# Conditioning in four blocks of 256 channels inside the first projections, and gates stored as nine rows

## The chip, the cores and the metric

The program runs on one NeuronCore of a Trainium2 chip. The metric is the device time of one execution in microseconds (us), the median of several runs. The engines are TensorE (PE in the rows; PEld is its weight load), VectorE (DVE), ScalarE (ACT), GpSimd (POOL) and SyncE (SP), each with a queue of its own, worked off in order. They wait for one another at semaphores.

## The reference

Two layers over a residual stream of width 1024, for one prompt of 1024 tokens and 8 samples of 16 tokens (1152 tokens, 9 tiles of 128). Before each of three stages the stream is normalized and modulated with a shift and a scale per sequence; the two layers also multiply their output with a gate per sequence. All come from a conditioning vector c (one for the prompt, eight for the samples: nine rows).

```
ada_mod(c, w, b)   = silu(c) @ w + b                     # w is 1024 x 3072: shift | scale | gate
modulate(x, g, shift, scale) = rms_norm(x, g) * (1 + scale) + shift
layer 0: h = modulate(x);  q, k, v, g = h @ w_in (1024 x 6144);  retention, head norm, * silu(g)
         x = x + gate * (o @ w_out)
shared:  h = modulate(x);  k, v, log forget gates = h @ kv_w
layer 1: h = modulate(x);  q, g = h @ w_in;  forgetting attention;  x = x + gate * (o @ w_out)
```

All weights are float32. A float32 product is done as three in float32r: each operand is a high part (rounded) and a low part (the rest), and hi·hi, hi·lo and lo·hi are added.

## The kernel before

**condition** (line 234) is a program block of its own with a barrier at its end. It clears c_rows and a bias tile on GpSimd (L280, L281), loads c and an identity, applies SiLU, transposes c to `pr.cT` (L309), and multiplies it with the shift and scale columns of a_ada_w: eight slices of 128 rows by 2048 columns (1 MB each, L273, four buffers), four products of 32 output rows for each slice, side by side in the array's column groups (L315). The bias is added (L332), four transposes turn the rows (L320), and `modulation` (L222) writes mod_b (shift) and mod_a ((1 + scale) times the norm's gain). The first weight chunk qk[0] is loaded between (`load_parts`, L167) and split into high (ScalarE, L196) and low (VectorE, L208). Then the nine x tiles come in (L276), ScalarE sums their squares (L301), and a root (L303) and a reciprocal (L340) give rstd for all nine.

**intake** (line 344) makes q, k and v of layer 0. GpSimd multiplies 128 channels of all tokens with rstd (L472) into one of two buffers xs. `turn(d)` on TensorE transposes them (L532, nine transposes) into PSUM, `modulated(d)` on VectorE applies mod_a and mod_b (L623 to L627) into ht, ScalarE casts ht to hT_hi (L499) and VectorE subtracts for hT_lo (L634). Turn 1 uses spare banks of another PSUM tensor, so turns 0 and 1 don't wait for each other. Meanwhile `products` (L542) of the first weight chunk run step by step over the eight d for AHEAD = 5 output tiles at once, in five PSUM banks. In this loop (L589) TensorE's queue has turn(d+2) first and then the products of d; VectorE's has modulated(d+1) and then the low part of d. After it come the other tiles of chunk 0 and seven more chunks, in the order of the code. The outputs go to DRAM scratch. From line 440 on, the rest of the conditioning (`side_steps`, L551) is done between these tiles: the gates of both layers and the shift and scale of the other two norms. SyncE waits for the last low part (L444) before it loads the rotary tables and the first side slices.

**Gates before.** `side_end(0)` after tile (4, 4) multiplies the nine gate rows with a table of zeros and ones, sel_gate (L578, eight products of 128x512), which repeats them for the 128 rows of a tile. VectorE copies each out (L677) and GpSimd stores it (L488) into the scratch tensor "gate" of (128, 2, 2, 1024). The trunk loads it with one transfer each for the prompt and the samples (L1025, L1039), the tail likewise (L1812, L1811).

The order of the queues is written out by hand; there is no planner.

Of the kernel before, what the change touches and what calls it, by code (L numbers as in the profile page):

```python
# [29 lines left out]
P = 128  # L30
# [23 lines left out]
def tables():  # L54
# [17 lines left out]
    sel_gate = np.zeros((P, 2, 4, P))  # L72
    for j in range(4):
        sel_gate[BR * j + DEC_BATCH, 0, j, :] = 1
        for b in range(DEC_BATCH):
            sel_gate[BR * j + b, 1, j, b * DEC_SEQ:(b + 1) * DEC_SEQ] = 1
# [9 lines left out]
    for r in range(2):  # L86
# [4 lines left out]
             sel_gate=sel_gate, sel_bias=sel_bias, mask=mask, sel_group=sel_group, mask_s=mask_s)  # L91
# [3 lines left out]
class Program:  # L95


    def __init__(self, nc, ctx, dram, table):
        self.nc, self.ctx, self.dram, self.table = nc, ctx, dram, table

        self.raw = self.sb("w_raw", [P, 2, KS, CW])
        self.w_hi = self.sb("w_hi", [P, 2, KT, CW], F32R)
# [6 lines left out]
        self.rstd_ready = self.sem("rstd_ready")  # L109
# [124 lines left out]
def condition(pr, x, x_rows, weight):  # L234


    nc = pr.nc
    dr = pr.dram
    xv = x[:, :].rearrange("p (t d) -> p t d", t=TILES)
    with ExitStack() as ctx:  # L240
        sb = lambda n, s, dt=F32: ctx.enter_context(nc.sbuf_tensor(n, s, dt))
        ps = lambda n, s: ctx.enter_context(nc.psum_tensor(n, s, F32))
        sem = ctx.enter_context(semaphores(nc, "ada_"))
        c_rows = sb("c_rows", [BR, D])
        c_silu = sb("c_silu", [BR, D])
        w = sb("ada_w_sb", [P, 4, 4, CW])
        bias = sb("ada_bias", [P, CW])
        rows = sb("ada_rows", [P, CW])
        squares = sb("squares", [P, 2, D])
        stat = sb("ada_stat", [P, 3, TILES])  # L250
        ps_c = ps("ps_c", [P, 512])
        ps_ada = ps("ps_ada", [P, 512])
        ps_t = ps("ps_t", [P, 512])
        in_landed, c_ready, b_zero, b_landed = sem("in_landed"), sem("c_ready"), sem("b_zero"), sem("b_landed")
        s_silu, c_turned, cT_ready = sem("s_silu"), sem("c_turned"), sem("cT_ready")
        w_landed = [sem(f"ada_landed{i}") for i in range(4)]
        x_landed = [sem(f"x_landed{i}") for i in range(3)]
        w_read, rows_ready, turned = sem("ada_read"), sem("rows_ready"), sem("ada_turned")
        sq_done, me_done, rt_done = sem("sq_done"), sem("me_done"), sem("rt_done")
        block = ctx.enter_context(nc.Block())  # L260

        @block.sync
        def _(sp):
            sp.wait_ge(c_ready, 1)
            sp.dma_start(c_rows[0:DEC_BATCH], dr["c_sample"]).then_inc(in_landed, 16)
            sp.dma_start(c_rows[DEC_BATCH:DEC_BATCH + 1], dr["c_prompt"]).then_inc(in_landed, 16)
            sp.dma_start(pr.ident[:, :], pr.table["ident"]).then_inc(in_landed, 16)
            for k in range(KT):
                if k >= 4:
                    sp.wait_ge(w_read, k - 3)  # L270
                if k == 4:
                    load_parts(pr, sp, weight, 0, 0)
                sp.dma_start(w[:, k % 4], dr["a_ada_w"][k * P:(k + 1) * P, 0:4 * CW].rearrange("p (j c) -> p j c", j=4)).then_inc(w_landed[k % 4], 16)  # L273
            load_parts(pr, sp, weight, 0, 1)
            for t in range(TILES):
                sp.dma_start(xv[:, t], x_rows(t)).then_inc(x_landed[t // 3], 16)  # L276

        @block.gpsimd
        def _(pool):
            pool.memset(c_rows[:, :], 0.0).then_inc(c_ready, 1)  # L280
            pool.memset(bias[:, :], 0.0).then_inc(b_zero, 1)  # L281
            pool.wait_ge(b_zero, 1)
            for j in range(4):
                pool.dma_start(bias[BR * j:BR * j + 9, :], dr["a_ada_b"][0:1, j * CW:(j + 1) * CW].to_broadcast([9, CW])).then_inc(b_landed, 16)
            with nc.allow_non_contiguous_dma(reason="channel gains, once"):
                for m, g in enumerate(("a_norm_g", "kv_norm_g", "b_norm_g")):
                    pool.dma_start(pr.norm_g[:, m, :], dr[g].rearrange("a (k p) -> p (a k)", p=P)).then_inc(b_landed, 16)
                pool.dma_start(pr.gn_g[:, :, :], dr["a_gn_g"].rearrange("a (n k p) -> p (a n) k", p=P, k=KT)).then_inc(b_landed, 16)

        @block.scalar  # L290
        def _(act):
            act.wait_ge(in_landed, 48)
            act.activation(c_silu[:, :], c_rows[:, :], ACT.Silu).then_inc(s_silu, 1)
            for sub in range(SUBS):
                split_hi(pr, act, 0, 0, sub)
            for t in range(TILES):
                if t % 3 == 0:
                    act.wait_ge(x_landed[t // 3], 48)
                if t:
                    act.wait_ge(sq_done, t)  # L300
                act.activation(squares[:, t % 2], xv[:, t], ACT.Square, accum_out=stat[:, 0, t:t + 1]).then_inc(sq_done, 1)  # L301
            act.wait_ge(me_done, 1)
            act.activation(stat[:, 2, :], stat[:, 1, :], ACT.Sqrt).then_inc(rt_done, 1)  # L303

        @block.tensor
        def _(pe):
            pe.wait_ge(s_silu, 1)
            for k in range(KT):
                ins = pe.transpose(ps_c[:, k * BR:(k + 1) * BR], c_silu[:, k * P:(k + 1) * P], pr.ident[0:BR, 0:BR])  # L309
            ins.then_inc(c_turned, 1)  # L310
            pe.wait_ge(cT_ready, 1)
            for k in range(KT):
                pe.wait_ge(w_landed[k % 4], 16 * (k // 4 + 1))
                for j in range(4):
                    ins = pe.matmul(ps_ada[BR * j:BR * (j + 1), :], pr.cT[:, k, :], w[:, k % 4, j, :],  # L315
                                    start=k == 0, stop=k == KT - 1, tile_position=(0, BR * j), skip_group_check=True)
                ins.then_inc(w_read, 1)
            pe.wait_ge(rows_ready, 1)
            for c in range(4):
                ins = pe.transpose(ps_t[:, c * P:(c + 1) * P], rows[:, c * P:(c + 1) * P], pr.ident[:, :])  # L320
            ins.then_inc(turned, 1)

        @block.vector
        def _(dve):
            dve.sem_inc(pr.raw_split, 2)
            dve.wait_ge(c_turned, 1)
            dve.tensor_copy(pr.cT[:, :, :], ps_c[:, 0:KT * BR]).then_inc(cT_ready, 1)
            for sub in range(2):
                split_lo(pr, dve, 0, 0, sub)
            dve.wait_ge(b_landed, 8 * 16)  # L330
            dve.wait_ge(w_read, KT)
            dve.tensor_tensor(rows[:, :], ps_ada[:, :], bias[:, :], ALU.add).then_inc(rows_ready, 1)  # L332
            dve.wait_ge(turned, 1)
# [1897 lines left out]
```

## Time and profile before

| | us |
|---|---|
| median of 3 runs (1793.59 to 1796.32) | 1795.57 |
| the profiled execution | 1794.28 |
| its span | 1792.5 |
| TensorE matmuls busy | 1724.7 (96%) |
| VectorE busy | 698.6 (39%) |
| ScalarE busy | 564.4 (31%) |
| GpSimd busy | 343.2 (19%) |

The span is the time from the first to the last instruction in the profiled execution; a busy share is taken of it. Rows give start and duration in us; a mean duration in a row of groups is in ns. The matmuls are pipelined, so the durations of two that follow each other overlap; the distance of their starts, or the chain of waits, tells what one costs. A float32 matmul (not float32r) is recorded as two instructions.

### The profile page before, as it was taken

What the parts mean: (1) busy time and instruction counts of PE and PEld (TensorE: products, weight loads), DVE (VectorE), ACT (ScalarE), POOL (GpSimd) and SP (SyncE); (2) the same over time, 40 slices, a digit from 0 to 9 for tenths busy, and PEclk for the clock granted to TensorE, in tenths of its full rate; (3) what the DMA queues carried; (4) which work ended last, traced back from release to release, by engine and by line L of the source; (5) the groups of instructions that cost most, each with busy time, mean ns of one, the idle gap of its engine ahead of it and who ended that gap; (6) DMA issues with size and microseconds to landing.
All of it is one profiled execution on the core that took longest, in us unless ns stands there. A gap on an engine that the chain in (4) does not pass through costs nothing.

```text
span 1792.5 us, 21860 instructions
## 1 busy us (share of the span) xinstructions
PE 1724.7 (96%) x8477; PEld 1325.6 (74%) x8477; DVE 698.6 (39%) x1429; ACT 564.4 (31%) x924; POOL 343.2 (19%) x413
## 2 busy tenths in 40 slices
PE   3699999999999999999999999999999998999998
PEld 0699998677876666666668888888788876777776
DVE  1654443211124444435433434645553115444432
ACT  2321111111133434434431224425222134344432
POOL 1311111100012323222222224404200000110000
PEclk9999999999999999999999999999999999999999
DMA  9064444542345645466562311332323645332200
GB/s 336 32 233 163 150 162 152 195 149 105 102 160 183 217 157 191 169 194 221 178 243 72 118 36 36 120 110 78 105 77 124 179 145 163 115 105 71 71 25 36
DMA packets 122568, 245.41 MB, mean 137 GB/s; under 512 B 15445, under 2 KB 50417, under 8 KB 121442
## 3 DMA queue, kind: packets, MB, share of 16 engines
q1 hardware_dynamic: 101202, 176.13, 30.8%
q0 software_dynamic: 21264, 67.88, 9.8%
q8 instruction: 68, 1.11, 0.3%
q14 instruction: 34, 0.28, 0.1%
HBM read 170.95 MB, written 73.02 MB: 136 GB/s over the span
## 4 chain that ended last, share of the span: by engine, by line
PE 93%; DVE 1%; ACT 1%; issue 1%; DMA 0%; POOL 0%; DVEq 0%; ACTq 0%; POOLq 0%
PE trunk_ps L1075 39%; PE in_ps_o L546 11%; PE in_ps_o L542 11%; PE tail_ps L1927 6%; PE tail_ps L1918 4%; PE tail_ps L1885 3%; PE trunk_ps L1101 3%; PE trunk_ps L1116 3%; PE tail_ps L1895 2%; PE trunk_ps L1111 2%; PE trunk_ps L1177 1%; PE tail_ps L1861 1%; PE in_ps_o L567 1%; PE trunk_ps L1145 1%; PE trunk_ps L1088 1%
## 5 line engine op out<-in xcount | busy, mean ns | idle before, releaser
L1075 PE MATMUL trunk_ps<-w_hi,hT_hi 128*128 128x512 f32 x1008 | 410.4, 407 | 0.0
L1075 PE MATMUL trunk_ps<-w_hi,hT_lo 128*128 128x512 f32 x1008 | 401.1, 398 | 0.0
L1075 PE MATMUL trunk_ps<-w_lo,hT_hi 128*128 128x512 f32 x1008 | 397.3, 394 | 0.0
L1075 PEld LDWEIGHTS trunk_ps<-w_hi,hT_hi 128*128 128x128 f32 x1008 | 189.3, 188 | 59.4 <-issue 17.6
L1075 PEld LDWEIGHTS trunk_ps<-w_lo,hT_hi 128*128 128x128 f32 x1008 | 189.5, 188 | 49.3 <-issue 5.0
L1075 PEld LDWEIGHTS trunk_ps<-w_hi,hT_lo 128*128 128x128 f32 x1008 | 189.2, 188 | 44.5
L208 DVE TENSOR_TENSOR w_lo<-w_raw,w_hi 128x1024 fp32r<-128x1024 f32 x80 | 101.6, 1272 | 296.3 <-ACT w_hi L196 291.1
L542 PE MATMUL in_ps_o<-hT_hi,w_hi 128*128 128x384 f32 x384 | 131.5, 342 | 4.6 <-DVE hT_lo L634 4.6
L542 PE MATMUL in_ps_o<-hT_hi,w_lo 128*128 128x384 f32 x384 | 130.0, 338 | 0.0
L542 PE MATMUL in_ps_o<-hT_lo,w_hi 128*128 128x384 f32 x384 | 130.0, 338 | 0.0
L546 PE MATMUL in_ps_o<-w_hi,hT_hi 128*128 128x512 f32 x288 | 115.2, 400 | 0.0
L546 PE MATMUL in_ps_o<-w_hi,hT_lo 128*128 128x512 f32 x288 | 113.9, 396 | 0.0
L546 PE MATMUL in_ps_o<-w_lo,hT_hi 128*128 128x512 f32 x288 | 113.2, 393 | 0.0
L196 ACT CAST w_hi<-w_raw 128x1024 fp32r<-128x1024 f32 x80 | 83.5, 1044 | 36.2 <-DMA w_raw<-in_a_w_in 36.2
L1410 POOL TENSOR_TENSOR room<-room 128x512 f32<-128x512 f32 x36 | 46.2, 1282 | 241.4 <-ACT room L1313 241.4
L1420 POOL TENSOR_TENSOR room<-room 128x512 f32<-128x512 f32 x36 | 56.4, 1568 | 139.9 <-DVE room L1601 139.9
L2016 ACT COPY tail_pT<-tail_ps 128x512 f32<-128x512 f32 (+3 forms) x104 | 46.3, 473 | 116.2 <-PE tail_ps L1895 116.1
L542 PEld LDWEIGHTS in_ps_o<-hT_hi,w_hi 128*128 128x128 f32 x384 | 72.8, 190 | 11.8 <-issue 10.3
L518 ACT COPY room<-in_ps_o 128x512 f32<-128x512 f32 x36 | 21.1, 587 | 184.9 <-PE in_ps_o L546 184.9
L2036 POOL TENSOR_TENSOR room<-room 128x512 f32<-128x512 f32 x16 | 20.2, 1264 | 279.1 <-DVE room L2125 279.1
L542 PEld LDWEIGHTS in_ps_o<-hT_lo,w_hi 128*128 128x128 f32 x384 | 72.9, 190 | 0.0
L542 PEld LDWEIGHTS in_ps_o<-hT_hi,w_lo 128*128 128x128 f32 x384 | 72.9, 190 | 0.0
(243 smaller groups left out, 2662.2 us busy)
## 6 DMA issues: line engine op xcount, KB each, us to landing
w_raw<-in_a_w_in SPq DMA_DIRECT2D x96, 256.0 KB, 3.0
room<-in_state_ret SPq DMA_DIRECT2D x64, 256.0 KB, 4.1
out_state_sample<-room POOLq DMA_DIRECT2D x64, 256.0 KB, 4.4
room<-in_b_ada_w SPq DMA_DIRECT2D x24, 512.0 KB, 6.2
scratch_qkT<-room POOLq DMA_DIRECT2D x48, 192.0 KB, 2.2
scratch_v<-room POOLq DMA_DIRECT2D x36, 256.0 KB, 2.6
room<-scratch_v SPq DMA_DIRECT2D x36, 256.0 KB, 4.4
scratch_o<-room POOLq DMA_DIRECT2D x36, 256.0 KB, 3.4
```

Source lines behind the costliest of these rows:

```text
L196: act.copy(pr.w_hi[:, slot, sub * KS:(sub + 1) * KS, :], pr.raw[:, sub % 2]).then_inc(pr.hi_done, 1)
L208: dve.tensor_tensor(pr.w_lo[:, slot, sub * KS:(sub + 1) * KS, :], pr.raw[:, sub % 2], pr.w_hi[:, slot, sub * KS:(sub + 1) * KS, :].bitcast ...
L542: ins = pe.matmul(ps_o[:, bank(c, t), 0:NB3], w[:, s, k, w0:w0 + P], h[:, k, n * NB3:(n + 1) * NB3], start=k + m == 0, stop=k == KT - 1 an ...
L546: ins = pe.matmul(ps_o[:, bank(c, t), :], h[:, k, t * P:(t + 1) * P], w[:, s, k, :], start=k + m == 0, stop=k == KT - 1 and m == 2)
L1075: ins = pe.matmul(ps[:, bank, :], h[:, k, t * P:(t + 1) * P], w[:, (C0 + j) % 2, k, :], start=k + m == 0, stop=k == KT - 1 and m == 2)
L1101: ins = pe.matmul(ps[:, PS_U + a, :], k_tok[:, c % 2, a * P:(a + 1) * P], v[:, n % 3], start=True, stop=True)
L1116: ins = pe.matmul(ps[:, PS_O, :], q[:, a, :], state[:, a, :], start=False, stop=a == 1)
L1420: pool.tensor_tensor(x1[:, t, cols_], x1[:, t, cols_], tmp[:, :], ALU.add).then_inc(added, 1)
L1885: ins = pe.matmul(ps[:, pair + a, 0:w], qT[:, s % 2, i, :], kT[:, n, a * CW:a * CW + w], start=True, stop=True)
L1918: ins = pe.matmul(ps[:, V, 0:DH], pT[:, x, y * P:(y + 1) * P], v_of(b)[:, n, :], start=b == 0, stop=b == blocks[u] - 1)
L1927: ins = pe.matmul(ps[:, bank, :], a[:, h, :], w[:, c, h, :], start=h + m == 0, stop=h == FH - 1 and m == 2)
L2016: act.copy(pT[:, x, 0:w], ps[:, TURN + place["p", u, x] % 2, 0:w]).then_inc(pt_ready, 1)
```

## The change

The block `condition` and its barrier are gone; intake does its work. The conditioning comes in four blocks m of 256 channels: the 256 shift and the 256 scale columns, side by side as 512, for all 1024 rows of the weight (2 MB, four transfers with runs of 1 KB), in two buffers that lie where the second weight chunk will be split to. One block is eight products: column group j sums k = j and k = 4 + j, and four small products with a 128x32 table "fold" add the groups and turn the rows at once. x is loaded first and scaled in place by VectorE, three tiles at a time. The splits of the first weight chunk into low parts go from VectorE to GpSimd. There is one PSUM buffer for turns, AHEAD is 4, and in the loop over d the turn stands behind the products. The gates are stored as nine rows, and the loads repeat them. Three pairs of semaphores are merged. What follows is the core.

```diff
+    "gate": (2, DEC_BATCH + 1, D)          # scratch, was (P, 2, 2, D)
-    AHEAD = 5
+    AHEAD = 4
+    BLOCK = 2 * P
@@ intake, sync
+            def ada_block(m):
+                if m >= 2:
+                    sp.wait_ge(*summed[m - 2])
+                for e in range(2):
+                    rows = slice(4 * e * P, 4 * (e + 1) * P)
+                    for h in range(2):
+                        cols = slice(h * D + m * BLOCK, h * D + (m + 1) * BLOCK)
+                        sp.dma_start(pr.ada[m % 2][:, 4 * e:4 * e + 4, h * BLOCK:(h + 1) * BLOCK],
+                                     dr["a_ada_w"][rows, cols].rearrange("(k p) c -> p k c", p=P)).then_inc(ada_in[m % 2], 16)
+            sp.wait_ge(*cleared)
...
+            for t in range(TILES):
+                sp.dma_start(xv[:, t], x_rows(t)).then_inc(x_in[t // 3], 16)
+            ada_block(0)
+            load_sub(pr, sp, chunks[0], 0, 0)
+            load_sub(pr, sp, chunks[0], 0, 1)
+            ada_block(1)
+            ada_block(2)
+            load_sub(pr, sp, chunks[0], 0, 2)
+            ada_block(3)
+            load_sub(pr, sp, chunks[0], 0, 3)
             load_parts(pr, sp, chunks[1], 1, 0)
@@ gpsimd
-            pool.wait_ge(pr.rstd_ready, 1)
-            for d in range(KT):
-                if d >= 2:
-                    pool.wait_ge(turned, d - 1)
-                pool.tensor_tensor(xs[:, d % 2]..., xv[:, :, d * P:(d + 1) * P], pr.rstd..., ALU.mult)
+            pool.wait_ge(*cleared)
...
+            for sub in range(SUBS):
+                split_lo(pr, pool, 0, 0, sub)
...
+                    if (c, t) == gates_at:
+                        pool.wait_ge(rows_read, 1)
+                        for j in range(4):
+                            dst = dr["gate"][j // 2, :, (j % 2) * CW:(j % 2 + 1) * CW].rearrange("b (a c) -> b a c", a=4)
+                            pool.dma_start(dst, side_rows[0][BR * j:BR * j + DEC_BATCH + 1]).then_inc(gate_stored, 16)
@@ scalar (squares of t wait for x_in[t // 3]; their output goes to PSUM)
+            for t in range(TILES):
+                squares(t)
+                if t in (3, 6):
+                    root(t // 3 - 1)
+            root(2)
+            for sub in range(2):
+                split_hi(pr, act, 0, 0, sub)
             for d in range(KT):
                 act.wait_ge(ht_ready, d + 1)
                 act.copy(hT_hi[:, d, :], ht[:, d % 2, :]).then_inc(hi_done, 1)
+                if d in (1, 3):
+                    split_hi(pr, act, 0, 0, 2 + d // 2)
@@ tensor
+            def ada(m):
+                pe.wait_ge(ada_in[m % 2], 64 * (m // 2 + 1))
+                if m:
+                    pe.wait_ge(*mods_out[m - 1])
+                for e in range(2):
+                    for j in range(4):
+                        ins = pe.matmul(ps_side[BR * j:BR * (j + 1), :], pr.cT[:, 4 * e + j, :], pr.ada[m % 2][:, 4 * e + j, :],
+                                        start=e == 0, stop=e == 1, tile_position=(0, BR * j), skip_group_check=True)
+            def fold_rows(m):
+                pe.wait_ge(*rows_out[m])
+                for a in range(4):
+                    ins = pe.matmul(ps_side[:, a * BR:(a + 1) * BR], ada_rows[:, a * P:(a + 1) * P], fold, start=True, stop=True, ...)
             def turn(d):
-                dst = turned_in(d)
-                pe.wait_ge(xs_ready, d + 1)
-                if d >= 2:
-                    pe.wait_ge(ht_ready, d - int(d == 2))
+                if d == 0:
+                    pe.wait_ge(*x_scaled)
+                else:
+                    pe.wait_ge(ht_ready, d)
@@ side_end
-                if r == 0:
-                    for n in range(8):
-                        if n >= 2:
-                            pe.wait_ge(g_read, n - 1)
-                        pe.matmul(ps_t[:, n % 2, :], sel_gate[:, n // 4, n % 4, :], side_rows[0], start=True, stop=True).then_inc(g_done, 1)
@@ tensor, main
+            ada(0)
+            fold_rows(0)
             turn(0)
             turn(1)
-            pe.wait_ge(pr.raw_split, SUBS + 2)
+            ada(1)
+            fold_rows(1)
             for d in range(KT):
+                pe.wait_ge(h_ready, d + 1)
+                pe.wait_ge(pr.raw_split, d // KS + 1 + 2)
+                for t in range(AHEAD):
+                    products(0, t, d)
+                if d in (1, 3):
+                    ada(2 + d // 2)
+                if d in (2, 4):
+                    fold_rows(1 + d // 2)
                 if d + 2 < KT:
                     turn(d + 2)
-                if d == 0:
-                    pe.wait_ge(ht_ready, 2)
-                pe.wait_ge(h_ready, d + 1)
-                for t in range(AHEAD):
-                    products(0, t, d)
@@ vector (rows: the bias; mods: mod_b and mod_a of two d; low: hT_lo)
+            dve.memset(c_rows, 0.0).then_inc(prepared, 1)
+            dve.memset(ada_bias, 0.0).then_inc(prepared, 1)
...
+            for g in range(3):
+                scaled_rows(g)
+            rows(0)
+            mods(0)
             modulated(0)
-            for d in range(KT):
+            modulated(1)
+            rows(1)
+            low(0)
+            mods(1)
+            for d in range(1, KT):
                 if d + 1 < KT:
                     modulated(d + 1)
...
+                low(d)
+                if d in (1, 3):
+                    rows(2 + d // 2)
+                if d in (2, 4):
+                    mods(1 + d // 2)
@@ trunk and tail, sync
-            sp.dma_start(gate[:, 1], dr["gate"][:, 0, 1]).then_inc(gate_in[1], 16)
+            for b in range(DEC_BATCH):
+                sp.dma_start(gate[DEC_SEQ * b:DEC_SEQ * (b + 1), 1], dr["gate"][0, b:b + 1, :].to_broadcast([DEC_SEQ, D])).then_inc(gate_in[1], 16)
-            sp.dma_start(gate_s[:, :], dr["gate"][:, 1, 1]).then_inc(gate_in, 16)
+            for b in range(DEC_BATCH):
+                sp.dma_start(gate_s[DEC_SEQ * b:DEC_SEQ * (b + 1), :], dr["gate"][1, b:b + 1, :].to_broadcast([DEC_SEQ, D])).then_inc(gate_in, 16)
```

## Rows read from the trace of the kernel before

**Rows 1.** First part of the page: busy time, share of the span, instructions.
```profile
PE 1724.7 (96%) x8477; PEld 1325.6 (74%) x8477; DVE 698.6 (39%) x1429; ACT 564.4 (31%) x924; POOL 343.2 (19%) x413
```

**Rows 2.** Chain of waits, 60 to 96 us: start, us, what.
```profile
62.25 3.20 DVE hT_lo L634
65.58 5.14 PE in_ps_o L542 x15
...
71.87 2.61 PE in_ps_o L542 x15
...
85.92 1.00 PE in_ps_t L532 x9
86.94 0.29 DVE room L623
87.24 0.98 DVE room L624
88.22 0.45 DVE room L625
88.67 0.20 DVE room L627
88.87 1.28 DVE hT_lo L634
...
90.19 5.86 PE in_ps_o L542 x31
```

**Rows 3.** Timeline, 0 to 62 us: start, us, engine, line, what, [idle before].
```profile
0.74 0.94 POOL L280 MEMSET c_rows<- 32x1024 f32 x1 [0.29 <-POOLq L2216]
1.63 0.52 POOL L281 MEMSET ada_bias<- 128x512 f32 x1
...
32.80 1.93 PE L315 MATMUL ps_ada<-ada_w_sb,cT 128*32 128x512 f32 x8 [0.58 <-DMA ada_w_sb<-in_a_ada_w]
34.88 0.69 DVE L332 TENSOR_TENSOR ada_rows<-ps_ada,ada_bias 128x512 f32<-128x512 f32 x1 [9.76 <-PE ps_ada L315]
35.63 1.11 PE L320 MATMUL ps_t<-ident,ada_rows 128*128 128x128 f32 x4 [0.89 <-DVE ada_rows L332]
...
50.76 1.28 ACT L303 ACT_TABLE_LOAD   x1
55.61 2.18 PE L532 MATMUL in_ps_t<-ident,room 128*128 128x128 f32 x9 [18.87 <-POOL room L472]
60.28 1.36 PE L532 MATMUL in_ps_t<-ident,room 128*128 128x128 f32 x9 [0.42 <-DVE room L627]
```

**Rows 4.** Stretches: busy us and count by engine, granted clock, DMA share, GB/s.
```profile
0.00:10.00 10.00, 2.12 (x16) 1.16 (x16) 0.42 (x1) 2.34 (x2) 7.70 (x14) 1.00 0.66 221
10.00:16.00 6.00, 2.81 (x15) 0.20 (x8) 0.00 (x0) 0.00 (x0) 0.00 (x0) 1.00 1.01 223
16.00:24.00 8.00, 3.87 (x16) 0.40 (x16) 1.33 (x2) 2.09 (x2) 0.00 (x0) 1.00 1.03 388
31.00:34.00 3.00, 2.42 (x16) 0.20 (x8) 0.00 (x0) 0.00 (x0) 0.00 (x0) 1.00 1.07 353
64.10:70.90 6.80, 5.32 (x17) 5.25 (x18) 4.53 (x6) 1.15 (x1) 0.12 (x1) 0.50 0.00 0
1494.30:1497.70 3.40, 1.72 (x14) 1.37 (x12) 2.24 (x10) 1.41 (x5) 0.00 (x0) 1.00 0.69 122
```

**Rows 5.** Groups of instructions by shape: count, busy us, mean ns.
```profile
L301 ACT ACTIVATE squares<-room 128x1024 f32<-128x1024 f32 x9 | 9.5, 1056 | 3.6 <-DMA room<-in_x_prompt 3.1 <-DMA room<-in_x_sample 0.3
L1375 POOL TENSOR_TENSOR room<-room,mod_b 128x1024 f32<-128x1024 f32 x16 | 37.3, 2329 | 45.7 <-DVE room L1536 45.7
```

**Rows 6.** Chain of waits, 300 to 345 us: the gate products.
```profile
321.18 0.87 PE in_ps_t L578 x2
...
329.23 11.20 PE in_ps_o L546 x48
```

**Rows 7.** SyncE's queue in the timeline: the load behind gate_s and gate in the tail.
```profile
1483.40 0.43 SPq L1778 DMA_DIRECT2D room<-out_v_prompt  x1
```

More of the change, by code:

```diff
@@ L71, in tables @@
                                EPS * np.exp(-2 * (i + 1.0) * g), EPS * np.exp(-2 * (loc + 1.0) * g)], 1) for g in lg], 1)
[L72 to L76, printed above, removed]
     sel_bias = np.zeros((4, 4, BR))
@@ L101, in __init__ @@
         self.raw = self.sb("w_raw", [P, 2, KS, CW])
+        with ExitStack() as below:
+            below.enter_context(nc.sbuf_tensor("below_w", [P, KT * CW], F32))
+            ada_0 = below.enter_context(nc.sbuf_tensor("ada_w0", [P, KT, CW], F32))
+            below.enter_context(nc.sbuf_tensor("between_w", [P, KT * CW], F32))
+            ada_1 = below.enter_context(nc.sbuf_tensor("ada_w1", [P, KT, CW], F32))
+        self.ada = [ada_0, ada_1]
         self.w_hi = self.sb("w_hi", [P, 2, KT, CW], F32R)
@@ L231, in modulation @@
     return ins
[L234 to L333, printed above, removed]
-            modulation(pr, dve, 0, ps_t[:, :])
-            for sub in range(2, SUBS):
-                split_lo(pr, dve, 0, 0, sub)
-            dve.wait_ge(sq_done, TILES)
-            dve.tensor_scalar(stat[:, 1, :], stat[:, 0, :], 1.0 / D, EPS, ALU.mult, ALU.add).then_inc(me_done, 1)
-            dve.wait_ge(rt_done, 1)
-            dve.reciprocal(pr.rstd[:, :], stat[:, 2, :]).then_inc(pr.rstd_ready, 1)
@@ L344, in intake @@
-def intake(pr, room, weights, after):
+def intake(pr, room, x_rows, weights, after):
     nc, dr = pr.nc, pr.dram
@@ L359, in bank @@
     def bank(c, t):
-        if c == 0 and t < AHEAD:
-            return t
         return t % 4 if c < ROT else t % 3
@@ L411, in intake @@
         side_tab, side_c_ready, side_used, rows_read = sem("side_tab"), sem("side_c_ready"), sem("side_used"), sem("rows_read")
-        g_done, g_read, side_turned, side_mod = sem("g_done"), sem("g_read"), sem("side_turned"), sem("side_mod")
-        gate_stored = [sem(f"gate_stored{i}") for i in range(3)]
-        def turned_in(d):
-            return ps_o[:, AHEAD - 3:AHEAD, :] if d == 1 else ps_t[:, :, :]
+        side_turned, side_mod, gate_stored = sem("side_turned"), sem("side_mod"), sem("gate_stored")
         def slot_of(c, t):
@@ L452, in _ @@
                 sp.dma_start(side_bias[:, r, :], dr[f"{m}_ada_b"][0:1, 0:4 * CW].rearrange("o (j c) -> (o j) c", c=CW)).then_inc(side_tab, 16)
-            sp.dma_start(sel_gate[:, :, :, :], pr.table["sel_gate"].rearrange("p (a b c) -> p a b c", a=2, b=4)).then_inc(side_tab, 16)
             for c in range(CHUNKS):
@@ L613, in _, with scaled_rows, rows, mods @@
         def _(dve):
+            def scaled_rows(g):
+                part = slice(3 * g, 3 * g + 3)
+                dve.wait_ge(*squared[g])
+                dve.tensor_scalar(stat[:, 1, part], stat[:, 0, part], 1.0 / D, EPS, ALU.mult, ALU.add).then_inc(prepared, 1)
+                dve.wait_ge(*root_of[g])
+                dve.reciprocal(pr.rstd[:, part], stat[:, 2, part]).then_inc(prepared, 1)
+                dve.wait_ge(*inverted[g])
+                for t in range(3 * g, 3 * g + 3):
+                    dve.tensor_scalar(xv[:, t], xv[:, t], pr.rstd[:, t:t + 1], None, ALU.mult).then_inc(prepared, 1)
+            def rows(m):
+                if m == 0:
+                    dve.wait_ge(bias_in, 6 * 16)
+                dve.wait_ge(*summed[m])
+                dve.tensor_tensor(ada_rows, ps_side, ada_bias[:, m, :], ALU.add).then_inc(prepared, 1)
+            def mods(m):
+                dve.wait_ge(*folded[m])
+                new = ps_side[:, 0:4 * BR].rearrange("p (a b) -> p a b", a=4)[:, :, 0:DEC_BATCH + 1]
+                dve.tensor_copy(pr.mod_b[0][:, 2 * m:2 * m + 2, :], new[:, 0:2])
+                for e in range(2):
+                    ins = dve.tensor_scalar(pr.mod_a[0][:, 2 * m + e, :], new[:, 2 + e], 1.0, pr.norm_g[:, 0, 2 * m + e:2 * m + e + 1], ALU.add, ALU.mult)
+                ins.then_inc(prepared, 1)
             def modulated(d):
-                z, src = ht[:, d % 2, :], turned_in(d)
+                z = ht[:, d % 2, :]
                 dve.wait_ge(turned, d + 1)
+                dve.wait_ge(*mods_out[d // 2])
                 if d >= 2:
```

140 lines of the change are left out of this document (85 added, 55 removed).

## Prediction

> **What bounds the kernel now.** I read the page's first part before anything else: matmuls are busy for 1724.7 us of 1792.5 [rows 1], so whatever stands still or is redundant on TensorE is what can be won. The chain of waits comes next, because it says where TensorE isn't what is waited for. Of the two places that this change touches, the first is the head of the program. TensorE does nothing that lasts before its first product of the projections at 65.58 [rows 2]; ahead of it lie, one after the other, the conditioning's eight loads and products (the last from 32.80), the squares, a root, the row scaling on GpSimd, and two sets of transposes from 55.61 [rows 3]. From 65.58 the eight steps d of the first five tiles run. The turn of step d+2 stands ahead of the products of step d, so VectorE works on the next step beneath the products: in the chain a step is almost wholly TensorE's (2.61 of products, 1.00 of transposes), and only for the last turn does VectorE's row of work come into sight, 86.94 to 90.15 [rows 2]. The last low part ends at 90.15, and 30 products of that phase are left from 90.19; at 0.174 us each (2.61 / 15) they end at 95.4. The second place is the gate expansion at 321: the chain leaves the value products at 321.18 and is back in them at 329.23 [rows 6].
>
> **Front of the program, step by step.** I rebuild the new order from rows of the old.
> *Clearing.* SyncE now waits for two clears on VectorE, 1024 and 2048 columns. VectorE clears nothing in this trace; the nearest rows are GpSimd's, 0.94 us for 1024 and 0.52 for 512 [rows 3], so about 3.1 us from 0.74: SyncE starts at 3.9, not at 1.7 behind the first clear alone, 2.2 us later. Bounds: half of it if VectorE clears twice as fast, and 3.1 as taken. The Trainium skill (VectorE: DVE Perf Modes, "Zero memsets can be issued as uint32 (trn2)") gives a clear one cycle per element whatever the type, which by its 0.96 GHz would be 3.2 us; no run here shows it yet.
> *x.* It is 4.7 MB and now comes first. The old stream had moved 2.2 MB by 10 us and 3.55 by 16 (223 GB/s while the gains' tiny elements are on the queues), then ran at 388 [rows 4]: 4.85 MB at 19.4, plus 2.2 for the late start is 21.6. Squares are 1.06 us each [rows 5], 1.2 with the readout of their sum (nine of them in 11 us); three can run only after the last third of x, with the root's table load (1.28) [rows 3] already behind: roots at 26.3, reciprocal, then three scalings on VectorE. A 128x1024 multiply by a column isn't in the trace; 768 columns out of PSUM took 0.98 [rows 2], so at most 1.3 each, and perhaps half: x is scaled by 28.5 to 30.5.
> *First block.* 2.1 MB in 1 KB runs at the 353 GB/s that 31 to 34 us shows, where the slices are mostly such runs [rows 4]: 21.6 + 5.9 = 27.5. Its eight products are two of the old groups of four (1.94 each) [rows 3]: 31.3, later than the scaling, which so costs nothing. Adding the bias 0.69, fold about 0.7 (the four transposes were 1.11), four small VectorE operations 0.65 to 0.7: the fold ends at 32.8 and turn(0), 2.18 us at the low clock level, at 35.0. Modulation is 0.29 + 0.98 + 0.45 + 0.20 in the old chain; two of its operations are merged, so 1.75: 36.8. turn(1) now has to wait for that, since there is one PSUM buffer: 39.1. Block 1 (27.5 + two slices of weights 3.0 + 5.9 = 36.4) is there; its products end at 43.0, bias 43.7, low part 1.28: the first projection product starts at **45.1**. All TensorE times in this are those of the 1.2 GHz level. At 2.4 GHz from turn(0) on it would be 41.8. I take 43.5, the middle: 22 us ahead of 65.58.
> *The eight steps.* Here the change gives most of it back. turn(d+2) now stands behind products(d). low(d) stands behind modulated(d+1) on VectorE, which needs turn(d+1), which stands behind products(d-1). So nothing overlaps: products 12 x 0.174 = 2.09, turn 1.00, modulation 1.75, low part 1.28, releases 0.05 = 6.15 us, six times = 36.9. Within it TensorE also gets blocks 2 and 3 (16 products, twice 1.9 at full clock: half of 3.87) and two folds (0.9 together). The bias additions and the mods on VectorE lie beside turns. The last two products take 4.2. Sum from 43.5: 43.5 + 36.9 + 3.8 + 0.9 + 4.2 = 89.3. One tile fewer is ahead than in the old phase: 24 x 0.174 = 4.2, so 93.5 against 95.4: **-1.9**, at the full clock.
> *GpSimd's four weight splits.* A 128x1024 of its own took 2.33 us [rows 5]; they end at some 47 and 63 us for the last two, between two low parts, so I cost them at nothing. If one meets a low part, the row is hT_lo at 3.20 in the chain beside GpSimd's scaling, against 1.28 alone [rows 2]: +1.9 each, bounds 0 and 3.8.
>
> **TensorE's clock in this phase.** TensorE idles for 0.05 + 1.75 + 1.28 + 0.05 = 3.1 us in each step. In the old trace it stood still from 61.6 [rows 3] to 65.6 and the granted clock was 0.50 from 64.1 to 70.9, the 1.2 GHz level; it was 1.00 again afterwards, and stayed there over pauses of 1 to 1.5 us, as in 1494.3 to 1497.7 with 1.72 us of products in 3.40 [rows 4]. A pause of 3.1 lies between these. A step at half clock costs 2.09 + 0.96 more, a block 1.9, a fold 0.45: 27 us if all are, 0 if none. But a step at the low level holds 6 us of unbroken TensorE work, as much as brought the level back in the old trace, so it should return about once a step. I take two of eight, **+6**.
> The Trainium skill warns here (TensorE: Matmul & The Clock Gate, "HAM oscillation — how this bites in real kernels"): a loop whose products are shorter than the wait behind them starts every round throttled. By that rule all eight steps would be slow; the old trace agrees only in that its one pause of 4 us did so. It is the second rival below.
>
> **The gates.** Eight products of 128x512 and the waits between them go: 329.23 - 321.18 = **-8.05** on the chain [rows 6]. The sel_gate load, eight copies and eight 256 KB stores go too, beside TensorE: nothing more. Four small stores take their place on GpSimd. Reading nine rows costs SyncE seven more issues for gate[:,1] and seven for gate_s, at the 0.43 us of the issue in [rows 7]: 3.0 us each on that queue. Queued behind the first are three x tiles that the residual needs much later, behind the second the values load at 1483.40 for the tail's next step. Bounds 0 and 6; I take **+0.5**, as both look covered.
> Merged semaphores and the moved PSUM bank cost nothing: same order, same instructions.
>
> **Sum.** -1.9 + 6 - 8.05 + 0.5 = -3.5 us. The profiled execution took 1794.28 (span 1792.5), so 1790.8; the median of the runs is 1795.57, 1.3 higher, and the changed kernel's median should be **1792.1**. About 0.2%, 3.6 us, is what a measurement of this kernel can tell from none.
>
> **Rivals.**
> *The clock stays up (0.22).* For it: the pause is shorter than the one that brought it down, and blocks 2 and 3 fill two steps. Then the start is 41.8 and nothing is added: -3.6 - 8.05 + 0.5 = -11.2, **1784.4**.
> *The clock drops in most steps (0.17), the slower side.* One mechanism, TensorE's 3.1 us pause. From a start of 45.1 the full-clock balance is -7.9, and each slow step adds 3.05: it turns to a loss with the third slow group and is a measurable one from the fourth. Five give +7.4, **1803**; all eight with blocks and folds 1815. Against it: 6 us of work in a row each time.
> *The blocks come late (0.16).* If 1 KB runs move at the 223 GB/s of 10 to 16 us instead of 353, block 0 lands at 31.0 and block 1, with the weight slices between, at 45.1; its products end at 49.0 instead of 43.0. That adds 6: **1798**. Against it: 223 was beside tiny elements, which are gone by then.
> Forecast itself: 0.45, own range 1788.5 to 1796.
>
> **How the numbers follow.** Faster: all of the first rival (0.22) and 0.24 of the forecast, which lies right at the bound; 0.46. Same: 0.21 of the forecast and 0.11 of the late blocks, 0.32. Slower: 0.17 and 0.05, 0.22. The range 1783 to 1802 holds the forecast, most of the first rival, nearly all of the third and half of the second.
>
> **What would show it.** First product at 41 to 46. Between product groups of the first eight steps: starts 6.2 us apart where granted clock is 1.00, about 9 where 0.50, with VectorE's modulated and low rows in the chain each time. Twelve products a group. No gate products between the value tiles. What would make it wrong: a low part beside a GpSimd split at 3 us, a first product after 47, a granted clock at one level throughout, or a wait in the tail on the later values load.

## The result: 9 us slower, and where they went

Five runs of the changed kernel gave a median of 1802.59 us (1797.13 to 1803.32), five of the kernel before, on the same chip, 1793.59 (1792.06 to 1796.32): a ratio of 1.0035, 95% interval 1.0019 to 1.0050. (The ratio is an estimate from all the runs; that of the two medians alone is 1.0050. The same holds for the ratios below.) I forecast 1792.1, 3.5 us faster; it is 9 us slower and just outside the range (1783 to 1802). The profiled execution is the fastest of the five (1797.13, span 1795.3), so a second profile stands beside it below, of a run at 1804.91 (span 1803.1), which is 1.3 us above the median of its own batch.

The first part of the page of after, the answer to [rows 1]:

```profile
PE 1720.6 (96%) x8489; PEld 1331.0 (74%) x8489; DVE 696.1 (39%) x1429; ACT 564.2 (31%) x926; POOL 331.4 (18%) x401
```

TensorE is busy 4 us less in a span that is 3 us longer, so it stands still more. The chain of waits of after, 28 to 125 us, answers to [rows 2]. Line numbers have moved: L512 is the old L542 (products), L502 the old L532 (turn), L484 a block's products, L492 the fold, L626 to L629 `modulated`, L634 the low part, L531 the first side step.

```profile
29.24 3.25 PE in_ps_o L484 x16
...
43.83 2.38 PE in_ps_o L512 x12
46.22 1.00 PE in_ps_t L502 x9
47.21 0.02 issue
47.23 0.29 DVE room L626
47.52 1.25 DVE room L627
48.78 0.53 DVE room L629
49.31 1.28 DVE hT_lo L634
50.59 0.04 issue
50.63 2.35 PE in_ps_o L512 x12
52.98 1.85 PE in_ps_o L484 x16
54.84 1.15 PE in_ps_t L502 x9
...
59.07 3.91 PE in_ps_o L512 x12
62.99 0.81 PE in_ps_o L492 x8
...
67.91 2.98 PE in_ps_o L512 x12
70.89 2.83 PE in_ps_o L484 x16
...
85.24 3.16 PE in_ps_o L512 x12
88.40 1.80 PE in_ps_t L502 x9
...
93.28 26.82 PE in_ps_o L512 x144
120.10 0.99 PE in_ps_o L531 x8
```

The serial step is there as drawn: products, turn, three operations of `modulated`, the low part, and only then the next products; of VectorE's work only a block's bias addition and mods lie beside TensorE's. What is new against the forecast is that the same twelve products take 2.35, 2.98, 3.16 or 3.91. The stretches say why. The last column but two is the granted clock; the last row is the whole loop, the other four are the half-clock stretches in and behind it, each 3.4 us (a fifth, 38.7 to 42.1, lies ahead of it):

```profile
59.10:62.50 3.40, 3.40 (x11) 3.40 (x12) 0.00 (x0) 0.78 (x1) 2.37 (x1) 0.52 0.00 0
69.40:72.80 3.40, 3.40 (x18) 1.58 (x20) 0.00 (x0) 0.00 (x0) 0.00 (x0) 0.51 0.00 0
86.40:89.80 3.40, 3.40 (x15) 3.31 (x15) 0.00 (x0) 0.00 (x0) 0.00 (x0) 0.52 0.00 0
93.30:96.70 3.40, 3.40 (x11) 3.40 (x12) 1.24 (x1) 0.00 (x0) 0.00 (x0) 0.51 0.31 96
43.80:93.30 49.50, 30.53 (x175) 24.58 (x175) 21.06 (x36) 8.91 (x8) 4.71 (x2) 0.90 0.25 81
```

Each step has a pause of 3.1 us, and where the clock falls it comes back within the same step, as forecast, but it falls more than twice: four times from 59 to 97 here. Three of the loop's six groups show it, the one at 59.07 from its start, those at 67.91 and 85.24 only 1.5 and 1.2 us in. A group that meets the whole stretch loses 1.56 (3.91 - 2.35).

Read at fixed places of the program, with the second profile of the changed kernel and the one of the experiment that holds the clock up (all in us from the span's start):

| | before | after | changed again | clock held up |
|---|---|---|---|---|
| first projection product | 65.6 | 43.8 | 47.3 | 45.6 |
| last two product groups begin | 90.2 | 93.3 | 99.5 | 90.0 |
| first side step | 112.5 | 120.1 | 126.7 | 115.2 |
| trunk's first product | 512.7 | 512.3 | 518.9 | 507.4 |
| tail's first transposes | 1463.1 | 1464.2 | 1470.9 | 1459.2 |
| tail's last output product begins | 1787.7 | 1790.5 | 1798.3 | 1784.9 |
| span | 1792.5 | 1795.3 | 1803.1 | 1789.7 |

The front of the changed kernel gains 18 to 22 us at the first product and has lost 8 to 14 at the first side step. From there to the trunk every kernel with the new gates takes 392.2 to 392.3 instead of 400.2: 8.0 us. Behind the trunk's start the changed kernel loses 1.6 us ahead of the tail and 1.7 to 2.9 in it. The profiles show half clock again there: 919.3 to 922.7 and 1496.1 to 1502.9 in after, 925.6 to 929.0 and 1502.5 to 1512.7 in the second profile, where the profile of before has none in either place.

### The profile page after: what moved, and what is told of

Read it like the earlier page. It is cut to its first block, busy times and chain, and to the rows that moved or that the text cites. A ratio compares the mean times of both kernels' runs of the same rounds, so it can differ in the third digit from the quotient of the medians.

```text
span 1795.3 us, 21868 instructions
## 1 busy us (share of the span) xinstructions
PE 1720.6 (96%) x8489; PEld 1331.0 (74%) x8489; DVE 696.1 (39%) x1429; ACT 564.2 (31%) x926; POOL 331.4 (18%) x401
## 4 chain that ended last, share of the span: by engine, by line
PE 94%; DVE 2%; ACT 1%; issue 1%; SPq 1%; DMA 1%; DVEq 0%; ACTq 0%
PE trunk_ps L1091 39%; PE in_ps_o L512 12%; PE in_ps_o L516 11%; PE tail_ps L1944 6%; PE tail_ps L1935 4%; PE tail_ps L1902 3%; PE trunk_ps L1117 3%; PE trunk_ps L1132 3%; PE tail_ps L1912 2%; PE trunk_ps L1127 2%; PE trunk_ps L1193 1%; PE tail_ps L1878 1%; PE in_ps_o L537 1%; PE trunk_ps L1161 1%; PE trunk_ps L1104 1%
## 5 line engine op out<-in xcount | busy, mean ns | idle before, releaser
L1091 PEld LDWEIGHTS trunk_ps<-w_hi,hT_hi 128*128 128x128 f32 x1008 | 189.8, 188 | 59.1 <-issue 17.5
L1091 PEld LDWEIGHTS trunk_ps<-w_hi,hT_lo 128*128 128x128 f32 x1008 | 189.6, 188 | 45.1
L208 DVE TENSOR_TENSOR w_lo<-w_raw,w_hi 128x1024 fp32r<-128x1024 f32 x76 | 96.8, 1275 | 282.9 <-ACT w_hi L196 277.7
L512 PE MATMUL in_ps_o<-hT_hi,w_hi 128*128 128x384 f32 x384 | 132.5, 345 | 19.1 <-DVE hT_lo L634 19.1
L512 PE MATMUL in_ps_o<-hT_lo,w_hi 128*128 128x384 f32 x384 | 130.9, 341 | 0.0
L512 PE MATMUL in_ps_o<-hT_hi,w_lo 128*128 128x384 f32 x384 | 130.9, 341 | 0.0
L512 PEld LDWEIGHTS in_ps_o<-hT_hi,w_hi 128*128 128x128 f32 x384 | 73.4, 191 | 26.6 <-DVE hT_lo L634 20.7
L1426 POOL TENSOR_TENSOR room<-room 128x512 f32<-128x512 f32 x36 | 46.3, 1286 | 241.4 <-ACT room L1329 241.4
L196 ACT CAST w_hi<-w_raw 128x1024 fp32r<-128x1024 f32 x80 | 83.5, 1044 | 13.4 <-DMA w_raw<-in_a_w_in 13.4
L1436 POOL TENSOR_TENSOR room<-room 128x512 f32<-128x512 f32 x36 | 56.5, 1568 | 141.4 <-DVE room L1617 141.4
L467 ACT COPY room<-in_ps_o 128x384 f32<-128x384 f32 x48 | 23.0, 481 | 161.5 <-PE in_ps_o L512 158.5
L512 PEld LDWEIGHTS in_ps_o<-hT_hi,w_lo 128*128 128x128 f32 x384 | 73.7, 192 | 0.0
L512 PEld LDWEIGHTS in_ps_o<-hT_lo,w_hi 128*128 128x128 f32 x384 | 73.6, 192 | 0.0
```

The lines of the kernel that those rows point to most:

```text
L196: act.copy(pr.w_hi[:, slot, sub * KS:(sub + 1) * KS, :], pr.raw[:, sub % 2]).then_inc(pr.hi_done, 1)
L208: dve.tensor_tensor(pr.w_lo[:, slot, sub * KS:(sub + 1) * KS, :], pr.raw[:, sub % 2], pr.w_hi[:, slot, sub * KS:(sub + 1) * KS, :].bitcast ...
L512: ins = pe.matmul(ps_o[:, bank(c, t), 0:NB3], w[:, s, k, w0:w0 + P], h[:, k, n * NB3:(n + 1) * NB3], start=k + m == 0, stop=k == KT - 1 an ...
L1091: ins = pe.matmul(ps[:, bank, :], h[:, k, t * P:(t + 1) * P], w[:, (C0 + j) % 2, k, :], start=k + m == 0, stop=k == KT - 1 and m == 2)
L1426: pool.tensor_tensor(o_t[:, n % 2], o_t[:, n % 2], g_t[:, :], ALU.mult).then_inc(gated, 1)
L1436: pool.tensor_tensor(x1[:, t, cols_], x1[:, t, cols_], tmp[:, :], ALU.add).then_inc(added, 1)
```

## Experiments

Seven kernels in two batches, each batch beside the kernel before on the same chip: 1793.86 (17 runs) for the first four, 1794.81 (7 runs) for the last three.

**The changed kernel again.** No edit.

> The changed kernel once more, for a second profile and more runs. Its first profiled run was 1797.1 and the median 1802.6, a spread of 6 us where the kernel before has 4. If that spread is TensorE's clock falling in other steps of the loop and later, this profile shows the same order and the same instructions with half-clock stretches in other places or of other length, and the time goes with the number of them, about 1.7 us for each stretch of 3.4 us in which TensorE is the one waited for.

1803.59 (1797.00 to 1805.60, 6 runs), ratio 1.0043 (1.0027 to 1.0058). The loss repeats. Its chain of waits:

```profile
29.30 3.68 PE in_ps_o L484 x16
...
33.82 1.91 PE in_ps_o L492 x8
...
41.73 3.56 PE in_ps_o L484 x16
...
47.32 3.27 PE in_ps_o L512 x12
...
55.36 3.87 PE in_ps_o L512 x12
...
65.32 3.91 PE in_ps_o L512 x12
...
74.16 2.35 PE in_ps_o L512 x12
...
82.60 3.91 PE in_ps_o L512 x12
...
91.43 3.09 PE in_ps_o L512 x12
...
99.50 27.24 PE in_ps_o L512 x144
```

Five of the six groups in the loop are slow in part, and so is the work ahead of it: the fold took 1.91 here and 1.08 at 33.34 in after. The loop took 52.2 us against 49.5 in after. It is the same program: how often the clock falls differs from one execution to the next. That the times, from 1797 to 1806, spread with it fits these two profiles; the other runs have none.

**The gate part alone, on the kernel before.** The whole gate part of the diff (four row stores on GpSimd for eight products, copies and stores; loads that repeat the rows), nothing of the conditioning:

```diff
-                if r == 0:
-                    for n in range(8):
...
-                        pe.matmul(ps_t[:, n % 2, :], sel_gate[:, n // 4, n % 4, :], side_rows[0], ...)
...
+                    if (c, t) == gates_at:
...
+                        for j in range(4):
...
+                            pool.dma_start(dst, side_rows[0][BR * j:BR * j + DEC_BATCH + 1]).then_inc(gate_stored, 16)
```

> The kernel before with the gate part of the change alone: nine rows stored, repeated by the loads, no expansion products. Theory A: the chain loses the 8.0 us between 321.2 and 329.2 and nothing else moves, so 8 us less than before, about 1785.5. Theory C (the additional loads on SyncE's queue and the reads of single rows cost what the products gave): 0 to 3 us less, 1791 to 1794.

1787.28 (1785.84 to 1788.19, 5 runs), ratio 0.9960 (0.9948 to 0.9972). That is 5 to 9 us of gain, 6.6 by the medians, with 392.3 us from the first side step (111.7) to the trunk (504.0): the 8.0 of the table. It is less than 8 in all because this profile too has half clock in the tail (6.8 us of it, 1486.4 to 1493.2), which takes 1.8 us longer than in before; so that isn't the new front's doing alone. The gates do what was forecast, and the rest of the change costs about 16 (1803.6 - 1787.3) where I had it at +4.

**Clock held up by filler products.** After, with 14 products of 128x384 behind each of the six turns, into a bank that is free then. They read what is there and are thrown away; they stand in the pause that TensorE has anyway:

```diff
...
+                    pe.wait_ge(*[mods_out[1], rows_out[2], mods_out[2], rows_out[3], mods_out[3], mods_out[3]][d])
+                    for _ in range(FILL):
+                        pe.matmul(ps_side[:, 0:NB3], pr.w_hi[:, 0, 0, 0:P], hT_hi[:, 0, 0:NB3], start=True, stop=True)
```

> The changed kernel with 14 products of 128x384 added behind each of the six turns in the loop, into a free PSUM bank; their result is not used. They fill 2.4 us of TensorE's pause of 3.4 us at the full clock. Theory A with the clock as its second part: the granted clock stays at 1.00 from the second step on, the steps lose their half-clock share, and the time falls by 5 to 7 us against the changed kernel, to about 1796, with less spread between runs; the serial order itself stays (steps of 6.8 us). If the clock has no part in it: 0 to +2 us, since the fillers only take up idle time.

1792.25 (1791.29 to 1795.79, 11 runs), ratio 0.9991 (0.9982 to 0.9999): 11.3 us under the changed kernel in the same batch, with more work in it. First the loop's stretch, then three pieces of the chain of waits:

```profile
45.60:90.00 44.40, 40.36 (x259) 35.01 (x259) 20.73 (x36) 8.91 (x8) 4.76 (x2) 1.00 0.25 80
```

```profile
45.61 2.35 PE in_ps_o L513 x12
...
62.84 0.81 PE in_ps_o L493 x8
...
89.98 25.23 PE in_ps_o L513 x144
```

The granted clock is 1.00 through the loop, against 0.90 in after and 0.84 in its second profile. The order of the work is untouched, so this prices the clock by itself. The two profiles of that batch differ by 13.4 (1804.9 and 1791.5): 1.7 ahead of the loop, where no filler stands, 7.8 in it (52.2 against 44.4), 2.0 in the 144 products behind (27.24 against 25.23), 1.9 later. So the clock in and behind the loop costs 9.8 in the second profile. In after it is 6.7 by the same two terms (49.5 and 26.82), with 0.33 of another cause in it (see GpSimd's splits below). And 44.4 us are what six steps cost at full clock, where I had 41.6.

**The turn ahead of the products again.** After, with turn(d+2) moved back in front of the products of d, one PSUM buffer and all else as in after:

```diff
+                if d + 2 < KT:
+                    turn(d + 2)
...
                 for t in range(AHEAD):
                     products(0, t, d)
...
-                if d + 2 < KT:
-                    turn(d + 2)
```

> The changed kernel with one edit: in TensorE's loop over d, turn(d+2) stands ahead of the products of d again, as in the kernel before. Theory A (the serial loop: products, turn, modulation, low part one after the other, 49.5 us for six steps in the changed kernel's chain): a step falls to what TensorE or VectorE needs alone, about 3.4 us and 5.3 where a block is in it, the first side step moves from 120 to about 101 us, and the time falls by 17 to 20 us, to 1783-1786. Theory B (TensorE's clock is the loss, the order only a side issue): only the 6 to 7 us of half clock inside the loop come back, 1796. Theory C (the loss lies behind the first phase, in the gates' reads and the tail): no change within 2 us.

1786.05 (1781.09 to 1790.00, 6 runs), ratio 0.9954 (0.9939 to 0.9969): 17.5 us under the changed kernel. One line's place turns a loss into a gain. It didn't restore the old overlap in full: blocks 2 and 3 still stand behind products(d) while VectorE's `rows` wait for them, and the clock still fell at 63.3, 73.6 and 80.4; the last two groups began at 86.3.

**The blocks pulled ahead too.** The kernel above, with ada(2) and ada(3) behind turn(d+2) but ahead of products(d), and the folds right behind products(d):

```diff
                 if d + 2 < KT:
                     turn(d + 2)
+                if d in (1, 3):
+                    ada(2 + d // 2)
...
                 for t in range(AHEAD):
                     products(0, t, d)
                 if d in (1, 3):
-                    ada(2 + d // 2)
-                if d in (2, 4):
-                    fold_rows(1 + d // 2)
+                    fold_rows(2 + d // 2)
```

> The previous experiment's loop still had VectorE waiting in four steps: the bias and the mods of blocks 2 and 3 stand behind products(d) in TensorE's queue and ahead of modulated(d+2) in VectorE's. Here the block's products stand behind turn(d+2) and ahead of products(d), the fold right behind products(d); all else as in the changed kernel. Theory A (queue order sets the step): each step is TensorE's own work, 3.3 us and 6.0 where block and fold are in it, the six steps take about 26 us instead of 49, the first side step stands at 98 to 100 us instead of 120 to 127, and the time is 1774 to 1777. Theory B (with the order mended, VectorE's 3.1 us a step and the clock bound it): steps of 4 us and more with half-clock stretches, 1781 to 1785, little less than with the turn ahead alone (1786).

1774.19 (1773.71 to 1776.72, 4 runs), ratio 0.9884 (0.9869 to 0.9899). The same work as after in another order on TensorE's queue, with the one PSUM buffer and the four tiles kept, 29 us faster by the medians of the two batches. Its chain of waits:

```profile
45.25 2.10 PE in_ps_o L512 x12
47.35 0.98 PE in_ps_t L502 x9
48.33 1.85 PE in_ps_o L484 x16
50.19 2.31 PE in_ps_o L512 x12
52.50 0.81 PE in_ps_o L492 x8
53.31 1.03 PE in_ps_t L502 x9
...
55.90 2.16 DVE room L629
...
71.53 25.23 PE in_ps_o L512 x144
```

Six steps take 26.3 us instead of 49.5, TensorE's pieces mostly follow one another, twelve products take 2.10 behind a turn and 2.31 behind a block, where they took 2.35 behind a pause, and the clock is 1.00. VectorE is in the chain twice: from 54.36 to 58.06, with 2.16 us for a 128x128 addition that is 0.20 elsewhere (see the last section), and from 65.31 to 71.48, the modulations and low parts of the last two d.

**The other way round: the turn last, on the kernel before.** The old program, five tiles ahead, two turns in separate banks, and nothing changed but the place of the turn:

```diff
-                if d + 2 < KT:
-                    turn(d + 2)
...
                 for t in range(AHEAD):
                     products(0, t, d)
+                if d + 2 < KT:
+                    turn(d + 2)
```

> The kernel before with one edit: the turn of step d+2 behind the products of step d, nothing else of the change. Theory A: the step becomes the serial sum, products 2.9, turn 1.0, modulation 2.0, low part 1.3 = 7.1 us instead of 3.7, six steps 42 instead of 24.6, so 18 us more at the full clock and up to 28 with half-clock stretches: 1812 to 1822. If the serial order alone is not the cost, but the blocks inside the loop are: under 5 us more, below 1799.

1828.22 (1826.14 to 1828.69, 4 runs), ratio 1.0180 (1.0165 to 1.0195), 33 us slower:

```profile
81.11 5.17 PE in_ps_o L542 x15
86.28 1.34 PE in_ps_t L532 x9
...
91.28 5.17 PE in_ps_o L542 x15
```

Six steps take 56.8 us (62.95 to 119.77) where [rows 2] has 24.6 (65.58 to 90.19): 32 of the 33. The order alone does it, without blocks, folds or a single PSUM buffer, and here all six groups of 15 are slow in part and three wholly, 5.17 against 2.61. In after the clock falls less often. The two differ in the blocks and folds, which lengthen the work of some steps, and also in the pause: 3.65 us in the first four steps here and 3.27 in the last two, against 3.09 in after. Neither was varied by itself, so which of them matters stays open.

**The first x tiles ahead of the clears.** The pipelined kernel with the first three x loads issued before SyncE waits for the two clears:

```diff
+            for t in range(3):
+                sp.dma_start(xv[:, t], x_rows(t)).then_inc(x_in[t // 3], 16)
             sp.wait_ge(*cleared)
...
-            for t in range(TILES):
+            for t in range(3, TILES):
```

> As the pipelined loop, and SyncE issues the first three x tiles before it waits for VectorE's two clears, which only the rows of c need. In the changed kernel SyncE's first transfer starts at 4.2 us and everything up to block 1 arrives one behind the other. If the front is bound by arrival, all of it moves 3 us up and the time is 3 us below the pipelined loop's, 1771 to 1774. If it is bound by VectorE's and TensorE's chain between the two blocks (turns, modulation), under 1 us.

1772.81 (1772.66 to 1773.83, 4 runs), ratio 0.9875 (0.9859 to 0.9892). The first side step comes at 95.7 instead of 96.8, 1.4 us by the medians; its interval overlaps that of the pipelined kernel, so that it is the better of the two is likely, not shown. The 3 us that I expected did arrive at the first block, which came at 26.0 instead of 29.7. But in this execution the fold and the first two turns ran at half speed (1.91, 1.99 and 2.18 us, where the pipelined kernel has 1.08, 1.03 and 1.20), and the first product came only 0.4 us earlier (44.89 for 45.25). It is the best version of the study, some 22 us under the kernel before and 31 under the changed one.

## Why the prediction was wrong, step by step

**What bounds it, and the mechanism: right.** I said that the loop becomes serial and gives most of the early start back. It did: the front won 18 to 22 us at the first product and gave back 29 to 33 by the first side step. Both one-line experiments put the cause in the turn's place.

**The start: at the upper bound.** SyncE started at 4.20 (forecast 3.9), x was scaled at 30.1 (28.5 to 30.5), the first block came at 29.1 instead of 27.5:

```profile
2.40 1.76 DVE L638 MEMSET room<- 128x2048 f32 x1 [0.38 <-issue]
...
22.16 2.08 DVE L598 TENSOR_SCALAR room<-room,rstd 128x1024 f32<-128x1024 f32 x3
...
28.01 2.08 DVE L598 TENSOR_SCALAR room<-room,rstd 128x1024 f32<-128x1024 f32 x3
```

(Timeline of after.) The profile of after gives 43.83 for the first product, as if the forecast 43.5 were confirmed; the two others with the same order up to there gave 45.6 (clock held up) and 47.3 (changed again); the latter is beyond the 47 that I had named as a sign of being wrong. I took the middle between all TensorE work at the low level (45.1) and all at the high one (41.8). In the second profile the blocks, the first fold and both turns are at the low level, with the block 1.6 late on top: +3.8. The durations say so, and not the column of the granted clock, which is at 1.00 over the same stretch:

```profile
35.74 1.99 PE in_ps_t L502 x9
...
39.55 2.18 PE in_ps_t L502 x9
```

```profile
30.00:43.80 13.80, 11.09 (x54) 6.31 (x50) 4.77 (x11) 3.51 (x4) 4.67 (x2) 1.00 1.10 348
```

So ahead of the loop this column doesn't always show the level. The first turn of the old front says the same: nine transposes take 2.18 us in before, where the column is at 1.00 (50 to 60 us), and 2.18 with the gates alone, where it is at 0.51.

**The step sum, "6.15 us, six times = 36.9": too short, +2.8.** All of it can be read in the kernel with the clock held up. Twelve products behind a pause take 2.35, not 12 x 0.174 = 2.09; 0.174 was measured within a chain of TensorE work, and behind a turn, in the pipelined kernel, the twelve do take 2.10 (six times 0.26, 1.6 us). The folds took 0.81 each, not 0.45 (0.7). A turn behind a block took 1.15 instead of 1.00 (two, 0.3). These make 2.6; gaps of 0.02 to 0.04 in each step are the rest. The modulation (1.25 + 0.29 + 0.20 = 1.74) and the low part (1.28) were right to 0.01. This is why the first rival (the clock stays up, 11.2 us faster) was out of reach as well: with the clock at 1.00 through the loop the kernel was 1.6 us under the one before.

**The step that failed: TensorE's clock, "I take two of eight, +6".** From the loop's start to the products behind it the clock fell four times in the shorter run and six times in the second profile, in five of the loop's six groups. It costs 6.7 us in the first, close to my 6, and 9.8 in the second (7.8 in the loop, 2.0 in the 144 products behind it). The same clock also fell where I had no term, 3.3 to 4.4 us more (below), and set part of the late start. My reason was that 6 us of unbroken work bring the level back within the step. In the changed kernel they do, but a later pause takes it down again. I had a row of recovery and no row of a 3.1 us pause, and let the one stand in for the other. Between 0 and 27, 6 was not far off by itself; but start, step sum and clock, each taken from the middle or the short side, all missed in the same direction.

The second rival (clock drops in most steps, 1803) comes nearest, by place and by time, though not by its own price: it had 3.05 for a step that is slow throughout, while the loss is 1.6 for each 3.4 us stretch; the start, the step sum and the half clock of trunk and tail make up the rest. That its number fits is in part luck. The Trainium skill (TensorE: Matmul & The Clock Gate, "HAM oscillation — how this bites in real kernels") describes a loop whose products are shorter than the wait behind them, and every round of it starts slow. The traces agree only in part: of six groups one starts slow in after and three in the second profile, where two more turn slow 1.1 and 1.4 us in; in the kernel before with its turn last it is five of six.

**The sum.** At the first side step I forecast +4.1 against before (-1.9 + 6), and the second profile has +14.2. The difference of 10.1 is the start 3.8, full-clock terms 2.8 and the clock 3.8 (9.8 - 6), 10.4 together. With 4.4 behind the trunk's start and 0.5 less for SyncE that is the whole miss of this profile: 10.6 slower than before, where I had 3.5 faster.

**Gates: right.** -8.0 against -8.05 up to the trunk, and 5 to 9 us by the runs. **SyncE's issues: nothing.** No wait on the later values load shows in the chain of the tail; the forecast had +0.5. **GpSimd's splits:** 0.33 in after (0.53 instead of 0.20 at 48.78), near the nought that I took.

**What I had no term for.** 3.3 us (after) to 4.4 (second profile) behind the trunk's start, which the profiles show together with half-clock stretches. The one at 919 or 925 costs about 1.6 us and stands at one place of the program, 406 to 407 us behind the trunk's first product. It has its like in most profiles with the new front, also in the pipelined ones (at 896 and 895), and in the kernel before with its turn last (950), which has the old front; not in that with the turn ahead of the products, nor in before or with the gates alone. So it isn't the new front as such; why it comes stays open. Those in the tail are of 3.4 to 10.2 us, differ from profile to profile and come with the old front too; before and the kernel with the turn ahead have none.

**The blocks come late (third rival): no.** Block 1 was there when its turn came (in the second profile its products follow the turn at once, at 41.73 in the chain), and no load stands in the loop's chain.

## What to carry to other kernels

When a change moves producer and consumer of a software pipeline in the queues, write the new chain of one round before anything else: whatever stands behind the products on TensorE but feeds the next round's VectorE work costs its whole length, and one line's place was worth 17 us here and 33 in the older kernel. Then look at the pause that this chain leaves on TensorE: price it in half-clock stretches for every round, not for some, and take the price of products behind a pause from such a place. And when an early start is won, see that what used to hide beneath it still has a cover; the same new front with its turns and blocks ahead of the products turned a loss of 9 us into a gain of 21.

## What the runs showed of the hardware

**A pause of 3.1 us in each round takes TensorE's clock down in some rounds and not in others.** With 3.4 to 5.4 us of full-clock work between the pauses the granted clock fell four times in one execution of the changed kernel and six times in another, at other steps, and was at the lower level for 3.4 us each time. Some of these falls came with the end of the pause, others 1.1 to 1.5 us later, when TensorE was at work again. With pauses of 3.27 to 3.65 us, in the kernel before with its turn last, it fell in all six steps, three times for 6.8 us. Fourteen products in each pause kept it at 1.00, and the extra work didn't lengthen the chain.

**A small VectorE addition waits for GpSimd.** Two rows of the pipelined kernel's timeline, of GpSimd and VectorE:

```profile
55.54 2.36 POOL L208 TENSOR_TENSOR w_lo<-w_raw,w_hi 128x1024 fp32r<-128x1024 f32 x1 [5.00 <-ACT w_hi L196]
```

```profile
55.82 2.23 DVE L629 TENSOR_TENSOR room<-room,mod_b 128x128 f32<-128x128 f32 x1
```

The 128x128 addition, both inputs in SBUF, begins 0.28 behind the split and ends 0.15 after it, 2.23 for what is 0.28 a step earlier (52.31). It ends about 0.15 behind a split in three more kernels too: after 0.62 us in after, 1.51 with the first x tiles ahead, 1.53 with the turn ahead. The 1024-column operation ahead of it, which reads PSUM, isn't held up: in after it lies wholly beneath the split of 46.82 to 49.16 and takes 1.33 (47.44). Where VectorE was first it was the split that took longer: 3.13 us at 47.41, beside the low part that had begun at 46.94. The Trainium skill (SBUF — State Buffer, "Who interferes with whom") has this as an exclusive lock between a VectorE operation with two SBUF inputs and a GpSimd one that reads SBUF; the trace agrees. In after only the end of such a split met the addition (0.33 us in the chain). In the pipelined kernel it is 1.96 us of the chain; a later split would be the next thing to try.

**A multiply by a column in SBUF is cheap.** 0.69 us for 128x1024 in place (2.08 for three), where I had allowed up to 1.3. VectorE cleared 2048 columns in 1.76 and 1024 in 0.91, so 0.86 to 0.89 ns a column and 2.67 us for both, less than either estimate in the prediction (3.1 and 3.2).
